# The start of a two-block transformer kernel: x loaded first, the decay product ahead of the projection chunks

## What is computed

```python
h = rmsnorm(x, norm_mix[0])
proj = h @ w_in                                   # 3072 columns of q, k, v; 1024 of z; 32 of a and b
qkv = silu(conv5(proj[:, :3072]))                 # over tokens, per column
q, k = l2norm(q) * DK ** -0.5, l2norm(k)          # 8 heads of 128
g = -exp(a_log) * softplus(a + dt_bias)           # decay, per token, head and direction
beta = sigmoid(b)
o = delta_rule(q, k, v, g, beta) + flipped one    # chunks of 128 tokens
o = o * rsqrt(mean(o * o) + eps) * norm_w * silu(z)
x = x + o @ w_out
```

## Time and profile before

| | us |
|---|---|
| median of 3 runs | 2462.5 (2462.17 to 2462.73) |
| the profiled execution | 2462.94 |
| its span, first to last instruction | 2460.9 |
| PE busy | 2001.7 (81%) |
| DVE busy | 929.5 (38%) |
| ACT busy | 631.4 (26%) |
| POOL busy | 32.6 (1%) |
| DMA over the span | 641.78 MB, 261 GB/s |

### The profile page before, as it was taken

How to read it: one execution, slowest core, us unless ns; L and a number is a source line. 1 busy time by engine, 2 the same in 40 slices (tenths; PEclk the granted TensorE clock), 3 DMA queues, 4 the chain that set the end, 5 groups by cost and what they waited for, 6 DMA issues and landing times.

```text
span 2460.9 us, 34473 instructions
## 1 busy us (share of the span) xinstructions
PE 2001.7 (81%) x14504; PEld 1369.6 (56%) x14504; DVE 929.5 (38%) x1671; ACT 631.4 (26%) x1058; POOL 32.6 (1%) x50
## 2 busy tenths in 40 slices
PE   7877788998988998899986666666999986666665
PEld 6756656886855787788852222222878852222222
DVE  4645564666644575554430000001554530000001
ACT  3222233441113443445340000000455330000000
POOL 0010000000000000000000000000000000000000
PEclk9979999998999999899988888888999988888887
DMA  8300023674954676441559999999641559999997
GB/s 318 107 1 35 3 104 134 242 267 161 381 213 161 218 260 231 159 168 38 239 215 426 428 426 427 426 426 414 243 156 64 221 236 426 426 426 426 426 426 325
DMA packets 150877, 641.78 MB, mean 261 GB/s; under 512 B 9374, under 2 KB 30904, under 8 KB 117622
## 3 DMA queue, kind: packets, MB, share of 16 engines
q1 hardware_dynamic: 144474, 637.13, 65.3%
q10 hardware_dynamic: 6300, 3.20, 0.4%
HBM read 639.21 MB, written 1.10 MB: 260 GB/s over the span
## 4 chain that ended last, share of the span: by engine, by line
PE 56%; DMA 32%; DVE 6%; ACT 3%; issue 1%; DVEq 1%; POOL 1%; SPq 0%; ACTq 0%; POOLq 0%
DMA ring<-in_w_down 32%; PE psum L1272 6%; PE psum L896 5%; PE psum L897 5%; PE psum L898 5%; PE psum L1405 4%; PE psum L994 3%; PE psum L668 2%; PE psum L1262 2%; PE psum L1151 2%; PE psum L1150 2%; PE psum L1152 2%; PE psum L699 1%; PE psum L1011 1%; PE psum L1141 1%
## 5 line engine op out<-in xcount | busy, mean ns | idle before, releaser
L1385 PE MATMUL psum<-ring,arena 128*32 128x256 f32 x4096 | 291.3, 435 | 184.7 <-DMA ring<-in_w_up 140.9
L1385 PEld LDWEIGHTS psum<-ring,arena 128*32 128x32 f32 x4096 | 142.1, 122 | 337.1 <-issue 147.8
L1405 PE MATMUL psum<-ring,arena 128*32 128x512 f32 x1024 | 165.1, 777 | 87.9 <-DMA ring<-in_w_down 78.7
L2159 DVE TENSOR_TENSOR arena<-psum,arena 128x256 f32<-128x256 f32 x32 | 13.6, 425 | 547.7 <-PE psum L1385 547.7
L896 PE MATMUL psum<-arena_r 128*128 128x512 f32 x512 | 207.5, 405 | 13.9 <-DVE arena_r L1768 7.1
L898 PE MATMUL psum<-ring_r,arena_r 128*128 128x512 f32 x512 | 204.7, 400 | 0.0
L1502 DVE TENSOR_TENSOR ring_r<-ring,arena_r 128x2048 fp32r<-128x2048 f32 x64 | 143.7, 2288 | 86.5 <-ACT arena_r L2220 86.5
L2166 DVE TENSOR_TENSOR arena<-psum,arena 128x512 f32<-128x512 f32 x64 | 44.3, 692 | 265.2 <-PE psum L1405 263.6
L2621 ACT ACTIVATE arena<-psum 128x256 f32<-128x256 f32 x32 | 12.3, 384 | 496.4 <-PE psum L1385 496.4
L2220 ACT CAST arena_r<-ring 128x2048 fp32r<-128x2048 f32 x64 | 119.5, 1903 | 72.7 <-PE psum L898 72.7
L1405 PEld LDWEIGHTS psum<-ring,arena 128*32 128x32 f32 x1024 | 32.8, 127 | 186.2 <-DMA ring<-in_w_down 95.9
(11 more groups left out here) (408 smaller groups left out, 3413.2 us busy)
## 6 DMA issues: line engine op xcount, KB each, us to landing
ring<-in_w_up SPq DMA_DIRECT2D x64, 2048.0 KB, 26.1
ring<-in_w_down SPq DMA_DIRECT2D x64, 2048.0 KB, 26.2
ring<-in_w_gate SPq DMA_DIRECT2D x60, 2048.0 KB, 26.7
ring<-in_mlp_w SPq DMA_DIRECT2D x32, 2048.0 KB, 7.9
ring<-in_w_mod SPq DMA_DIRECT2D x24, 2048.0 KB, 11.0
ring<-in_w_in SPq DMA_DIRECT2D x20, 2048.0 KB, 8.6
ring<-in_gdn_w_in SPq DMA_DIRECT2D x8, 2048.0 KB, 18.2
ring<-in_dswa_w_in SPq DMA_DIRECT2D x9, 1536.0 KB, 13.6
```

Source lines behind the costliest of these rows:

```text
L1385: ins = mm(PS[32 * j:32 * j + 32, 4 + m, 0:T], XGE[:, 4 * u + kk, :], W(v + 2 * m + u, D)[:, kk, j * T:(j + 1) * T], start=u == 0 and kk = ...
L1405: ins = mm(PS[32 * j:32 * j + 32, (7, 4)[half], :], HTE[:, k % 2, 32 * (k // 2):32 * (k // 2) + 32], W(v + 4 + u, D)[:, j, half * 512:(hal ...
```

## The change

Six things are done together.

1. SP issues x first of all. The parameter rows land in the arena (`ROWS_IN`, in the place of `KN`), no longer in the second half of `XN`, so that the norm can write there. `DTB` and `ALOG` are issued behind the rows and count as parameters (12 transfers in `PARAMS`).
2. ACT and DVE begin with the norm; ACT copies the parameter columns behind its scaling of x, and DVE waits for them only before it writes `HT`. The silu of `c_2` moves behind the first exponentials.
3. The ring numbers become `U_AB` 0, qkv 1 to 6, z 7 and 8. The decay product stands ahead of chunk 0 on PE.
4. On DVE the logits, the masks and the angles stand ahead of convolution 0, the steps of decay behind convolution 1, the totals behind convolution 7. On ACT the exponentials stand ahead of chunk 0.
5. The sums stand behind chunk 5 on PE.
6. The keys are scaled on DVE behind chunk 21. POOL waits for the square sums itself and adds eps itself. PE turns the keys around the last turns of chunks, and ACT copies them around its last silu.

```diff
-U_QKV, U_Z, U_AB, U_GOUT = 0, 6, 8, 9
+U_AB, U_QKV, U_Z, U_GOUT = 0, 1, 7, 9
...
+            sp.dma_start(X[:], A["x"][0].rearrange("(t p) d -> p t d", p=P)).then_inc(sem("x_in"), 16)
             sp.dma_start(base[:], A["k_base"]).then_inc(sem("params_in"), 16)
...
-            sp.dma_start(X[:], A["x"][0].rearrange("(t p) d -> p t d", p=P)).then_inc(sem("x_in"), 16)
-            load(0, cols(A["gdn_w_in"][0], 0, 512))
+            sp.dma_start(DTB, A["gdn_dt_bias"].rearrange("a b c -> a (b c)").partition_broadcast(P)[:, 0]).then_inc(sem("params_in"), 16)
+            sp.dma_start(ALOG, A["gdn_a_log"].rearrange("a b c -> a (b c)").partition_broadcast(P)[:, 0]).then_inc(sem("params_in"), 16)
+            load(U_AB, cols(A["gdn_w_in"][0], 4096, 4128))
+            load(U_QKV, cols(A["gdn_w_in"][0], 0, 512))
...
-            pe.wait_ge(sem("params_in"), 16 + 16 * sum(len(g) for g in ROWS))
+            pe.wait_ge(sem("params_in"), PARAMS)
...
+            decay_rows()
             for ch in range(24):
                 qkv(ch)
                 if ch >= 2:
                     turn(ch - 2)
+                if ch == 5:
+                    decay_sums()
+            pe.wait_ge(sem("gs_ready"), 2)
+            keys_turn(0)
+            keys_turn(1)
             turn(22)
+            keys_turn(2)
+            keys_turn(3)
             turn(23)
...
             pe.wait_ge(sem("knt_done"), 4)
+            pe.wait_ge(sem("tok_done"), 16)
             pe.wait_ge(sem("chunk_out"), 24)
...
+            decay_logits()
+            masks_and_angles()
             for ch in range(24):
                 conv(ch)
                 if ch - 3 >= GH:
                     to_tokens(ch - 3)
+                if ch == 1:
+                    decay_steps()
+                elif ch == 7:
+                    decay_totals()
+                elif ch == 21:
+                    keys_scaled()
...
+            decay_exps()
+            a.activation(CACT[:], COLS[:, COL["c_2"]:COL["c_2"] + 8], ACT.Silu).then_inc(sem("cact"), 1)
             for ch in range(24):
                 conv_in(ch)
                 if ch >= 1:
                     silu(ch - 1)
                 if ch >= 3 and ch - 3 < 16:
                     squares(ch - 3)
+            keys_back(0)
+            keys_back(1)
             silu(23)
...
-            pool.wait_ge(sem("gdn_ms"), 1)
+            pool.wait_ge(sem("sq_done"), 16)
+            flat_k = RQK.rearrange("p a b -> p (a b)")
+            g.tensor_tensor(flat_k, flat_k, eps[:].to_broadcast([P, 32]), ALU.add)
+            g.drain()
```

More of the change, by code:

```diff
@@ L401, in colof @@
             return COLS[:, COL[name] + i:COL[name] + i + 1]
+        PARAMS = 16 * (3 + sum(len(g) for g in ROWS))
         block = ctx.enter_context(nc.Block())
@@ L686, in turn, with decay_rows, decay_sums, keys_turn @@
                 ins.then_inc(sem("turned"), 1)
+            def decay_rows():
+                full(pe, U_AB)
+                for t in range(TT):
+                    for k in range(KC):
+                        ins = mm(PS[:, 6, t * 32:(t + 1) * 32], HT[:, k, t * P:(t + 1) * P],
+                                 ring[U_AB % RING][:, k * 32:(k + 1) * 32], start=k == 0, stop=k == KC - 1)
+                used(ins, U_AB)
+            def decay_sums():
+                pe.wait_ge(sem("gs_ready"), 1)
+                for d in range(2):
+                    rhs = GS[:, :, d * 8:(d + 1) * 8]
+                    mm(PS[:, 6, d * 16:(d + 1) * 16].rearrange("p (a b) -> p a b", b=8), CUM[:, d, :], rhs, start=True, stop=True)
+                    ins = mm(PS[:, 6, 32 + d * 16:48 + d * 16].rearrange("p (a b) -> p a b", b=8), ones, rhs, start=True, stop=True)
+                ins.then_inc(sem("knt_mm"), 1)
+            def keys_turn(g):
+                if g == 1:
+                    pe.wait_ge(sem("decay_in"), 2)
+                elif g >= 2:
+                    pe.wait_ge(sem("knt_done"), g - 1)
+                for hh in range(2):
+                    for t in range(TT):
+                        ins = nc.tensor.transpose(pair(7 - g % 2, P)[:, hh * 2 + t], KN[:, 2 * g + hh, t, :], ident)
+                ins.then_inc(sem("knt_mm"), 1)
+            decay_rows()
             for ch in range(24):
@@ L2252, in squares, with decay_exps, keys_back @@
                 a.copy(ajunk[:], RQK[:, 1, ch:ch + 1]).then_inc(sem("sq_done"), 1)
+            def decay_exps():
+                act.wait_ge(sem("decay_in"), 1)
+                s2 = [SPT[:, i, :].rearrange("p (t c) -> p t c", c=16) for i in range(6)]
+                a.activation(s2[2], s2[1], ACT.Exp)
+                a.activation(s2[4], PS[:, 6, 0:64].rearrange("p (t c) -> p t c", c=32)[:, :, 16:32], ACT.Exp, scale=-1.0)
+                a.activation(ALOG, ALOG, ACT.Exp)
+                settle()
+                a.activation(s2[3], s2[2], ACT.Ln, bias=1.0).then_inc(sem("decay_out"), 1)
+            def keys_back(g):
+                act.wait_ge(sem("knt_mm"), 1 + g + 1)
+                a.copy(KQT[:, 2 * g:2 * g + 2, 0, :], pair(7 - g % 2, T)).then_inc(sem("knt_done"), 1)
+            decay_exps()
+            a.activation(CACT[:], COLS[:, COL["c_2"]:COL["c_2"] + 8], ACT.Silu).then_inc(sem("cact"), 1)
             for ch in range(24):
```

180 lines of the change are left out of this document (77 added, 103 removed).

## The result

The changed kernel takes **2444.35 us** (median of 7 runs, 2442.32 to 2455.03), the kernel before 2462.5 (7 runs, 2459.14 to 2472.26). The ratio is 0.9933, 95% interval 0.9917 to 0.9949: 18 us less, where 15.5 were forecast (2447.0, range 2442.5 to 2452). Of that, the traces place what the steps up to the core gave beyond the forecast: 1.6 us in one profile and 2.6 in another.

The account below looks back on a forecast made before the run. Prediction: mostly TensorE bounds the kernel, a third is weight transfers, so front gains shift everything; -19.8 (tail) + 3.4 (start) + 0.9 (sums) = -15.5 us against 2462.94, giving 2447.4, as median 2447.0; range 2442.5 to 2452.

Parts of the forecast that it names:

- Tail: Stretch from the last projection chunk into the core's opening: 19.8 us gained, range 18.3 to 21.4.
- my two cases: Tail with PE at half clock, 18.3 us gained, or at full clock with a shorter core opening, 21.4.
- the middle value: Tail gain taken between the half-clock and full-clock figures: 19.8 us.
- Start: Program start: x turned 3.5 us earlier, but with the decay product ahead the first chunk starts 3.4 us later.
- x first gains 3.5: Start: with x issued first, PE turns it at 9.8 instead of 13.31, 3.5 us gained.
- Sums: Four sum products behind chunk 5, where PE is the bound: 0.9 us lost at full clock, 1.7 at half.
- POOL beside DVE: Rival: POOL's power and DVE's two-operand convolution steps hold each other off, costing 3.5 us: 2450.5; chance 0.12.
- Late parameters: Rival: parameters land late at the start, tail and sums at half clock: 2452.0 us; chance 0.10.
- slower: Rival: DVE's first convolution waits for late transfers, the positions last: some 2468 us or more; chance 0.03.
- The price I gave for that wait: DVE's wait for the positions before its first convolution: each microsecond past about 28 delays convolution 0.
- the rival of an absorbed gain: Behind the changed code, a later DMA wait with its own clock swallows the gain: 2462.5 us; chance 0.05.
- The rival of a warm start and tail: Transposes of x and decay product raise PE's clock: at most 2440 us, likelier half of it 2443.3; chance 0.15.

Follow-up runs that it names:

- copies_first: Changed kernel with each loop step's token copy of chunk ch - 3 ahead of convolution ch on DVE instead of behind it: 2444.57 us, one run.
- x_first_alone: Kernel before with only the transfer of x moved to the front of the queue: 2467.74 us, ratio 1.0011.
- x_behind: Changed kernel with x's transfer put back behind all the small ones, the norm still first on ACT and DVE: 2453.56 us, one run.
- before_again: Kernel before, unaltered, run once more for a second profile: 2467.36 us.
- long_powers: Changed kernel with ten more POOL powers of 32 elements beside the convolutions of chunks 2 to 14: 2446.81 us, one run.
- decay_in_chunks: Changed kernel with the decay product moved behind chunk 2, its logits, exponentials and sums moved back with it: 2455.04 us, ratio 0.9955.
- chunks_masks: Changed kernel with the decay product behind chunk 2, its followers later too, and masks and angles behind convolution 4: 2440.83 us, one run.
- free_start: Changed kernel with five matmuls on zeros before the parameters, two before the decay product, masks and angles behind convolution 4: 2442.28 us, ratio 0.9909.

## Why the prediction was right, point by point

- **Tail, 19.8 us forecast (18.3 at half clock, 21.4 at full).** In the first profile 25.89 - 7.39 = 18.5, and 1.65 from the opening: 20.15. In the second 19.8 and 1.66: 21.4, which is the full-clock case as forecast. The first profile is neither of my two cases. I had tied the shorter opening to a full clock in the tail, but here the clock was at half in the second part of the tail and full in the opening, and copies_first has the reverse: a tail at full clock, an opening at half, 6.32 us. That the middle value came within 0.4 us of the first profile is partly luck. The distances 7.4 and 6.1 from the copy to the core were right to 0.01 us, since every step in them had a row; single steps were off by more (PE's gap ahead of turn 22 was 1.55 us, not 0.6, as the first groups ran at full clock and then waited for DVE). All these gains are against the first profile of before; its second one (25.46 and an opening of 7.64) makes them 21.0 and 22.3.
- **Start, 3.4 us lost forecast.** 2.6 and 2.9 against the first profile of before, 1.6 and 1.9 against the second, whose slow beginning was 3.3. x was turned at 9.41, not 9.8, as the parameters landed at 8.53, not 8.9. Product and slow beginning together took 8.8 us in both profiles (6.02 + 2.78, and 7.04 + 1.73), where I had 6.9 + 2.07 = 9.0. The sum was close, the two terms were not in the first profile: the product was 0.9 us shorter, its beginning being at full clock, and the slow beginning 0.7 longer. I had put these in as two fixed costs, and they are one stretch at half clock that runs across both. Its end isn't fixed either: it was 26.0 in the first profile, and in the second the chunks were at full pace before that.
- **"x first gains 3.5"** gave the right time for a reason told too shortly. The old 5.43 us behind the landing of x were carried over as if the norm waited for x alone. That is true in the changed kernel, where ACT and DVE take x ahead of the columns. Neither half gains by itself: the transfer alone has x turned 1.0 us later than before (x_first_alone), the order alone 1.6 later (x_behind), both together 3.9 earlier.
- **Sums, 0.9 us forecast.** PE spends 0.81 on them (44.88 to 45.69), but from the end of chunk 2 to the copy of chunk 23 it is 84.27 and 84.28 us, 83.78 and 83.77 in the two profiles of before: 0.5. The other 0.4 is a delay that the kernel before has and the changed kernel doesn't. In both profiles of before, and in x_first_alone, one turn waits 0.91 us for ACT where its neighbours, and those of the changed kernel, wait 0.53:

```profile
96.63 0.41 PE L685 MATMUL psum<-base,arena 128*128 128x128 f32 x2 [0.91 <-ACT act_junk L2252]
```

That delay goes back to an idle time of 0.46 us on DVE inside one convolution (93.43 in before_again), for which the profile names no releaser. So the cost of the sums was right, and 0.4 us were gained that no term of mine had; why the new order is rid of them stays open.
- **POOL beside DVE** was rightly given the smaller chance, and long_powers settles it.
- **Late parameters** and **slower** did not occur. DVE's convolution 0 waits for ACT, 0.25 us, not for a transfer. But DVE did wait for the positions ahead of the masks, 1.66 and 0.91 us, where I had it free to go on, and in the second profile convolution 0 follows the angles without a wait. The price I gave for that wait, nothing before 28, holds only because the decay product keeps PE until 20.6: decay_in_chunks had the wait open, and it cost 2.8 us and the clock.
- **Sum.** 0.8 + 0.4 + 0.35 us is what the first profile had more than the sum of 15.5, so 17.05 at DVE's first product; 18.06 in the second. The gain reached the end of the program undiminished in the medians (18 us), so the rival of an absorbed gain is out. The rival of a warm start and tail came half true in the second profile, in the tail alone.

What stays open: in which of the two levels the clock stands in the tail differs from execution to execution of the same program, and I can't say what decides it. Nor did I find in which instruction the 7 us of the first profile's long second part were lost. About 3.8 of them lie between POOL's norm at 1955.55 and its last one at 2445.52 (490.0 us, 486.2 in the second profile), where the DMA queues are busy nearly throughout.

## What to carry to other kernels

A step on a serial stretch between two phases can often be put into the first phase for the price of what it costs the engine that is the bound there; price it at the clock level of the new place, look at what an engine does just before it, since a gap there can halve its pace, and look at what the engine would have waited for without it, since such a wait makes it cheaper. A transfer moved to the front gains nothing until the engines that consume it also take it first. And when an engine waits in a regular pattern, look for an operation that is queued behind one that waits for something later: swapping two lines on DVE was worth 7.2 us up to the core, beside 18 for the whole change.

## What the runs showed of the hardware that I had not expected

- A POOL power of 128x32 elements took 5.44 us beside two-operand steps of DVE (103.48 in the changed kernel) and 5.45 with DVE idle. Ten of them left DVE's steps at 484 ns (long_powers).
- Eight transposes of 128x128 by PE took 1.04 us at a granted clock of 1.00 and 1.91 at 0.50. The decay product took 109 ns an instruction at 1.00 (chunks_masks) and 209 at 0.50 (decay_in_chunks).
- Behind nine matmuls on zeros the transposes of x took 1.97 us instead of 3.38. The pace held across the gap of 1.83 us behind them, and the granted clock fell only at 18.9, in the product. In decay_in_chunks it was 1.00 ahead of a gap of 2.83 us and 0.50 behind it. In free_start it fell with no gap at all.
- At the program's start the granted clock in the records isn't to be relied on: in the second profile of the changed kernel it reads 1.00 while the product runs at 220 ns an instruction, as slow as at 0.50 in decay_in_chunks.

```profile
18.00:19.00 1.00, 1.00 (x6) 1.00 (x6) 0.00 (x0) 0.00 (x0) 0.00 (x0) 1.00 0.84 321
```
